# Moving one decode sequence's key pages out of the attention stage and into the chunk stage, with the magnitude on ScalarE

## What is computed

```python
z = einsum('bqhd,bkhd->bhqk', q, k) * SB_SCALE + bias
log_stay = where(valid, log_sigmoid(-z), 0)
log_after = reversed_cumsum(log_stay) - log_stay
a = where(valid, exp(log_sigmoid(z) + log_after), 0);  o = a @ v
```

## Time and profile before

| | us |
|---|---|
| three runs | 1563.23, 1570.99, 1570.99 |
| median | 1570.99 |
| profiled execution, its own time | 1570.6 |
| its span | 1568.9 |
| TensorE busy | 1422.8 (91%) |
| VectorE busy | 790.2 (50%) |
| ScalarE busy | 499.0 (32%) |
| GpSimd busy | 147.2 (9%) |

### The profile page before, as it was taken

The page is one execution under the profiler, slowest core; times in us unless marked ns, Lnnn a source line. Parts: engine busy times, 40 slices in busy tenths (PEclk is TensorE's granted clock), DMA queues, the critical chain, the costliest instruction groups (busy, mean ns, idle before and its releaser), DMA issues.

```text
span 1568.9 us, 28016 instructions
## 1 busy us (share of the span) xinstructions
PE 1422.8 (91%) x10682; PEld 1297.5 (83%) x10682; DVE 790.2 (50%) x2996; ACT 499.0 (32%) x768; POOL 147.2 (9%) x228
## 2 busy tenths in 40 slices
PE   5979978779999888969998899998989999999998
PEld 4979955458988788949776788898989999999997
DVE  4578749986998746553335422234243323332222
ACT  3323343326855322321213433123232222232211
POOL 1000011122320433110330000000000000000000
PEclk9989989889999977876988999998999999999999
DMA  9369846654544200029889998933223333332222
GB/s 323 99 205 291 274 177 201 199 182 146 187 115 115 68 21 21 15 68 267 289 296 310 360 366 294 325 98 126 68 68 92 88 92 93 95 91 82 80 78 75
DMA packets 254474, 252.57 MB, mean 161 GB/s; under 512 B 22433, under 2 KB 215083, under 8 KB 254309
## 3 DMA queue, kind: packets, MB, share of 16 engines
q1 hardware_dynamic: 254341, 250.79, 50.1%
HBM read 235.66 MB, written 15.29 MB: 160 GB/s over the span
## 4 chain that ended last, share of the span: by engine, by line
PE 75%; DVE 11%; ACT 4%; DMA 4%; POOL 2%; issue 2%; SPq 1%; POOLq 0%; DVEq 0%; ACTq 0%
PE ps L1017 53%; PE ps L1046 3%; PE ps L1105 2%; DVE kring L2045 2%; PE ps L1116 2%; PE ps L1390 1%; PE ps L1290 1%; DMA wring<-in_w_ffn_out 1%; PE ps L1307 1%; PE ps L1409 1%; PE ps L1280 1%; PE ps L1294 1%; PE ps L1058 1%; DMA kring<-in_cache_v 1%; SPq L718 1%
## 5 line engine op out<-in xcount | busy, mean ns | idle before, releaser
L1017 PE MATMUL ps<-obT_split,wring_split 128*128 128x268 f32 (+2 forms) x1296 | 264.7, 286 | 0.0
L1017 PE MATMUL ps<-obT_split,qv_split 128*128 128x260 f32 (+2 forms) x1040 | 219.1, 292 | 17.2 <-DVE wring_split L579 15.7
L579 DVE TENSOR_TENSOR wring_split<-wring,vring_split 128x1024 fp32r<-128x1024 f32 (+1 forms) x92 | 110.6, 1202 | 232.5 <-ACT vring_split L573 232.1
L1017 PEld LDWEIGHTS ps<-obT_split,wring_split 128*128 128x128 f32 (+1 forms) x1296 | 201.5, 189 | 0.7
L1017 PE MATMUL ps<-xn_split,vring_split 128*128 128x260 f32 (+1 forms) x960 | 194.6, 284 | 4.1 <-DVE obT_split L593 4.1
L1017 PE MATMUL ps<-obT_split,vring_split 128*128 128x260 f32 (+1 forms) x960 | 197.4, 287 | 0.8 <-issue 0.8
L1017 PEld LDWEIGHTS ps<-obT_split,qv_split 128*128 128x128 f32 (+1 forms) x1040 | 162.2, 190 | 41.6 <-issue 37.4
L1017 PE MATMUL ps<-xn_split,qv_split 128*128 128x260 f32 (+2 forms) x912 | 186.6, 286 | 0.0
L1577 ACT ACTIVATE R<-ps 128x520 f32<-128x520 f32 (+1 forms) x86 | 52.5, 611 | 375.5 <-PE ps L1017 375.5
L579 DVE TENSOR_TENSOR wring_split<-wring,qv_split 128x1024 fp32r<-128x1024 f32 (+1 forms) x73 | 91.8, 1258 | 146.0 <-ACT qv_split L573 145.9
L1017 PEld LDWEIGHTS ps<-xn_split,vring_split 128*128 128x128 f32 x960 | 149.0, 190 | 4.8 <-issue 4.2
(11 more groups left out here) (387 smaller groups left out, 2185.6 us busy)
## 6 DMA issues: line engine op xcount, KB each, us to landing
kring<-in_cache_k SPq DMA_DIRECT2D x74, 512.0 KB, 4.9
wring<-in_w_in SPq DMA_DIRECT2D x72, 512.0 KB, 5.3
vring<-in_cache_v SPq DMA_DIRECT2D x64, 512.0 KB, 6.1
kring<-in_cache_v SPq DMA_DIRECT2D x64, 512.0 KB, 5.5
wring<-in_w_ffn_in SPq DMA_DIRECT2D x44, 512.0 KB, 3.9
vring<-in_cache_k SPq DMA_DIRECT2D x30, 512.0 KB, 4.9
R<-in_cache_k SPq DMA_DIRECT2D x24, 512.0 KB, 6.8
wring<-in_w_ffn_out SPq DMA_DIRECT2D x16, 512.0 KB, 4.1
```

Source lines behind the costliest of these rows:

```text
L579: nc.vector.tensor_tensor(fr(w_part(wlo[:, p % RING, :], p)), w_part(wring[:, p % RING, :], p), w_part(w_high(p), p), ALU.subtract).then_i ...
L1017: last = mm(ps[0:m, 2 * (t % 2) + i, 0:n], fr(w), fr(x[k][:, a + i * n:a + i * n + n]), start=(k == 0 and w is w_h and x is hi), stop=(k = ...
```

## The change

Sequences 1 to 5 go by the plan, so that the attention scores 30 pages instead of 44 and segment 4 none. The seventh sequence (b = 6) is scored inside the chunks on VectorE, at places named in `CHUNK_PAGES`; its query is broadcast into `wring` slot 1 and its pages land in slots 2, 3 and 0, after the last tile of segment 4 has used them. The three weight tiles that would have been prefetched there are loaded after the sequence's last page is scored. The magnitude in the attention becomes an Abs on ScalarE.

```diff
-K_PLAN += [(("att", i), 3 - (i % 4 == 3)) for i in range(2 * H)]
+K_PLAN += [(("att", i), 2 - (i % 8 == 7)) for i in range(2 * H)]
 K_PLAN += list(zip([(2, q) for q in range(4)], (2, 0, 3, 3))) + list(zip([(3, q) for q in range(4)], (2, 2, 2, 2)))
-K_PLAN += list(zip([(4, q) for q in range(4)], (1, 1, 0, 0)))
+K_CHUNKS = PAGES * (DB - 2)
 K_END = PAGES * (DB - 1)
-assert _n == K_END
+assert _n == K_CHUNKS
+
+CHUNK_PAGES = {("levels", 0, 0): [0], ("levels", 0, 1): [1], ("levels", 0, 2): [2, 3], ("kv", 0): [4],
+               ("levels", 1, 1): [5], ("levels", 1, 2): [6, 7], ("levels", 2, 1): [8], ("levels", 2, 2): [9, 10],
+               ("kv", 2): [11], ("levels", 3, 1): [12], ("levels", 3, 2): [13, 14], ("kv", 3): [15]}
@@ k_slot, k_view
+    if n >= K_CHUNKS:
+        return (n - K_CHUNKS) % 3
+            if n >= K_CHUNKS:
+                return wring[:, (2, 3, 0)[k_slot(n)], :]
@@ SP
-                if p == 6 and b + 2 < DB:
+                if p == 6 and b + 3 < DB:
                     spread_q(b + 1)
+            def chunk_query():
+                sp.wait_ge(w_used, done(T_Z - 1))
+                sp.dma_start(wring[:, 1, :], qdram[DB - 2:DB - 1, :].to_broadcast([P, D])).then_inc(qb_in[DB % 2], 16)
+            def chunk_pages(a, b):
+                for p in range(a, b):
+                    k_page(DB - 2, p)
-                    if T_SEG + t + 3 < T_O:
+                    if T_SEG + t + 3 < T_Z or s >= 5 and T_SEG + t + 3 < T_O:
                         w_load(sp, T_SEG + t + 3)
                 if s == 4:
+                    chunk_query()
+                    chunk_pages(0, 3)
                     get_inverse(1)
+                    chunk_pages(3, 6)
                     late_query()
                     get_inverse(2)
+                    chunk_pages(6, 8)
+                    late_page(0)
+                    chunk_pages(8, 10)
                     last_inverse()
-                    late_page(0)
                     get_inverse(3)
+                    chunk_pages(10, 14)
                     late_page(1)
+                    chunk_pages(14, PAGES)
                     late_page(2)
+                    sp.wait_ge(k_used, K_END)
+                    for p in range(T_Z, T_Z + 3):
+                        w_load(sp, p)
                     v_quad(0)
@@ ScalarE, attend
                 def softplus(h):
+                    act.wait_ge(s_z, h + 1)
+                    if h:
+                        act.wait_ge(s_sp, h)
+                    go(es, zs[h % 3], ACT.Abs).then_inc(s_abs, 1)
                     act.wait_ge(s_abs, h + 1)
                     go(es, es, ACT.Exp, scale=-1.0).then_inc(s_exp, 1)
@@ ScalarE and GpSimd, first chunk
-                        act.wait_ge(k_used, K_END)
+                        act.wait_ge(k_used, K_CHUNKS)
-            pool.wait_ge(k_used, K_END)
+            pool.wait_ge(k_used, K_CHUNKS)
@@ VectorE, attend
-                    v.scalar_tensor_tensor(es, zs[h % 3], -1.0, zs[h % 3], ALU.mult, ALU.max).then_inc(s_abs, 1)
-                    for b, p in K_PAGES["att", 2 * h]:
-                        k_page(b, p)
-                    if h + 2 < H:
-                        magnitude(h + 2)
-                    for b, p in K_PAGES["att", 2 * h + 1]:
+                    for b, p in K_PAGES["att", 2 * h] + K_PAGES["att", 2 * h + 1]:
                         k_page(b, p)
@@ VectorE, chunks: levels(c)
+                    pages("levels", c, 0)
                     for g in G2:
                         after("pe", c, "up", 32, g)
                         ue, te = odd(U[:, hs(g), :], 32), even(T[:, hs(g), :], 32)
                         v.tensor_tensor(ue, ue, product(g, 32, 0), ALU.subtract).then_inc(g_dve, 1)
                         v.tensor_tensor(te, te, product(g, 32, 256), ALU.subtract).then_inc(g_dve, 1)
+                        pages("levels", c, 1 + g)
+                def pages(*key):
+                    for p in CHUNK_PAGES.get(key, ()):
+                        k_page(DB - 2, p)
@@ VectorE, chunks: loop over c
+                    pages("kv", c)
                     for g in G2:
                         after("pe", c, "kv", g)
```

More of the change, by code:

```diff
@@ L2043, in k_page @@
                     kh = k_head(n, h)
-                    qh = key_columns(0)[:, h, :] if n >= K_END else qbc[:, b % 2, h * P:h * P + P]
+                    if n >= K_END:
+                        qh = key_columns(0)[:, h, :]
+                    else:
+                        qh = (qbc[:, b % 2, :] if n < K_CHUNKS else wring[:, 1, :])[:, h * P:h * P + P]
                     m = v.tensor_tensor_reduce(kh, kh, qh, 1.0, 0.0, ALU.mult,
@@ L2093, in attend @@
             def attend():
-                def magnitude(h):
-                    dve.wait_ge(s_z, h + 1)
-                    if h == 0:
-                        dve.wait_ge(k_out[0], 16 * 8)
-                        dve.wait_ge(k_out[1], 16 * 4)
-                    if h >= 1:
-                        dve.wait_ge(s_sp, h)
-                    v.scalar_tensor_tensor(es, zs[h % 3], -1.0, zs[h % 3], ALU.mult, ALU.max).then_inc(s_abs, 1)
                 def softplus(h):
@@ L2113, in attend @@
                 for h in (0, 1):
-                    magnitude(h)
                     softplus(h)
```

## The result

The changed kernel took **1551.69 us** (median of 8 runs, 1549.70 to 1557.36); the kernel before, timed beside it, 1563.44 us (8 runs, 1560.78 to 1570.99). The ratio is 0.9914, with a 95% interval of 0.9887 to 0.9941: 11.8 us by the medians, 13.4 by the ratio. Timed once more as one of the experiments, it came to 0.9921 [0.9895, 0.9947].

What follows compares the result with a forecast made beforehand. It took TensorE to bound the kernel (75% of the span), with time to be had only where it stands still. From 1570.6 us, -11.2 - 1.1 - 3.0 + 2.7 = -12.6 gave 1558.0 us, range 1549 to 1571.

Steps and rivals of the forecast that it cites:

- Terms 1 and 2: Attention: fewer pages and the magnitude on ScalarE bring six turns from 91.63 to 80.4 us, -11.2 us.
- the ring: Attention: one head's loop through VectorE, GpSimd, ScalarE and TensorE to the next head's subtraction, 13.4 us instead of 15.27.
- the slack of 1.5 us on both engines: Attention: VectorE and ScalarE would each finish a head's work 1.5 us before the next subtraction is due.
- rival A: Attention: the clock falls anyway and turns stay at about 15.3 us; 1569.2 us, no change; chance 0.10.
- term 1: Attention: pages per head fall from 5.5 to 4, freeing at least 10.2 us of VectorE over six turns.
- Term 3: Start of attention: the first mask shortens once VectorE's magnitude goes, -1.1 us (bounds 0.3 and -1.4).
- Term 4: Fifth weight segment: two pages of the seventh sequence leave VectorE, -3.0 us (bounds -2.0 and -3.6).
- the cap is TensorE's longer wait: Fifth weight segment: the gain could not exceed TensorE's longer wait for VectorE's low parts, 3.6 us.
- Term 5: Chunks: sixteen pages enter VectorE's waits, some reduces slowed by GpSimd's multiplies, +2.7 us, +2.5 of it in chunk 0.
- B: Chunks: page loads come late and VectorE sits waiting at a page; 1572.5 us at worst; chance 0.17.
- C: Chunks: all pages land whole on the chain, 27.2 us in place of 2.7; 1582.5 us, slower; chance 0.08.
- D: Attention: the magnitude's move does nothing because ScalarE becomes the late engine; 1558 to 1568 us; chance 0.05.

Runs made afterwards that it cites:

- e10: The kernel before with only the magnitude moved to ScalarE, plus unread matmuls in TensorE's attention waits (two calls for heads 0 to 5, five after); 1553.04 us.
- e11: The changed kernel with the magnitude back on VectorE, plus unread matmuls in TensorE's attention waits (two calls for heads 0 to 5, five after); 1552.50 us.
- e2: The changed kernel with the magnitude back on VectorE, so only the pages are moved; 1554.30 us.
- e1: The kernel before with only the magnitude moved to ScalarE, all pages left in their places; 1554.72 us.
- e3: The changed kernel with 28 instead of 30 pages in the attention and two back in segment 4; 1556.64 us.
- e8: The kernel before with only the magnitude moved to ScalarE, plus too many unread matmuls in TensorE's attention waits (six calls, twelve for the last two heads); 1577.09 us.
- e4: The changed kernel with one reduce instead of eight for each page in the chunks, all loads and waits kept; 1547.83 us.
- e5: The whole changed kernel timed once more, as one of the experiments; 1551.23 us.
- e9: The changed kernel plus unread matmuls in TensorE's attention waits (two calls for heads 0 to 5, five for 6 and 7); 1546.36 us.
- e6: The changed kernel with chunk pages from page 3 on one place later and the first value pages' loads ahead of the three weight loads; 1550.73 us.
- e12: The changed kernel with chunk pages from page 3 on one place later, plus unread matmuls in TensorE's attention waits (two or five calls); 1545.34 us.

## Why the prediction was right, and where it was off

It said 1558.0 us (1549 to 1571) and faster; it was 1551.7 and faster. The change was foreseen at -12.6 us and is -11.8 by the medians, -13.4 by the ratio. The 6.3 us between 1558.0 and 1551.7 are almost all in the base: **the sum was made against the profiled execution of 1570.6 us, which the prediction took to stand 0.4 us under the median**. With eight runs instead of three the median was 1563.4. From there, -12.6 gives 1550.8.

The nearness of -12.6 is in part luck. With the sizes that are found below (attention -9.9, start -1.9, segment 4 -4.7, chunks +3.8) the sum is -12.7: four terms were off by 0.8 to 1.7 us each, and the errors cancel. The sizes come from single traces, and the kernel before has only the trace of a long execution, so this sum is no proof of the time either.

*Terms 1 and 2, attention: -11.2, and -11.4 in the trace.* The turn of the ring, the slack of 1.5 us on both engines, Abs at 1.32 us without a table load, the 2.21 us of idle and the 2.82 us product all stand in the rows. Two things were not seen. The two parts are not needed together: each alone gives turns of 13.36 to 13.9 us (e10, e11). And the fast product after 2.21 us is not certain, as "every turn is the 13.4 one with the idle of 2.21 and the fast L1116" had it: 7 of 42 were slow, at some 1.55 us each, so that the term in a mean execution is nearer -9.9 (one slow product in six). That is a part of rival A, which was given as all or nothing. One sum of term 1 is too small, though nothing was built on it: the plan takes ten pages out of the six turns, 17 us and not "at least 6 x 1.70 = 10.2"; with six magnitudes that is 26.3 us, and VectorE's busy time fell by 86.04 - 60.74 = 25.3.

The Trainium skill (TensorE: Matmul & The Clock Gate, A second HAM failure mode: psum-queue depth-cycling) describes a neighbouring case: in a bf16 kernel that cycles through PSUM banks, frequent short idles between groups of matmuls make the clock go back and forth between its two levels. Here the idle is a wait for ScalarE's exponential, in fp32, and the trace agrees: 2.21 us of idle in each turn and the clock lost in some. That it is the idle that does it is shown by the filled kernels.

*Term 3, start: -1.1, and -2.0.* The mask fell to 1.19 us as foreseen. The first subtraction starts at 227.40 to 227.86 us in the three traces with the magnitude on VectorE (before, e2, e11) and at 225.03 to 227.06 in the eleven with it on ScalarE, 1.9 us apart on average. So the term was 0.8 us too small by the averages; what the rest consists of was not followed.

*Term 4, segment 4: -3.0, and -4.7 in this pair of traces.* The step that failed there is "the cap is TensorE's longer wait", with "late next is VectorE still, for the last tile". Both waits went. The parts: the second page with its scaling 2.0 us, as worked out. The loads, foreseen "some 1 us sooner", came 1.0 us sooner in SP's queue and 1.9 us sooner in landing. VectorE's first elimination step follows the start of its last L579 by 469.27 - 467.13 = 2.14 us instead of 485.37 - 480.50 = 4.87; these 2.7 us and the 2.0 make 4.7. So "by itself it saves nothing" was right for the first page's reduces, and its place in the DMA queues was the larger part.

The other traces bear this out, with smaller numbers. In the five kernels with two pages in segment 4 (before, e1, e3, e8, e10) the step comes 5.2 to 6.5 us after the last matrix's issue, in the nine without 4.3 to 4.8. TensorE's waits for the low parts there are 4.9, 2.9, 3.6, 3.2 and 2.8 us, 3.5 on average, and none in the nine: the trace of before shows the largest. But in e1, e8 and e10 the clock also fell to its lower level (0.51) within 1.2 us of that wait's end, for 6.9, 6.9 and 3.5 us, and in no kernel without these pages did it fall there. The prediction had put the clock at nothing in this term.

*Term 5, chunks: +2.7, and +3.4 in chunk 0, +0.4 behind it (e4 against after).* L2318 is 1.7 us later in the trace, not 2.5. But the page ahead of the first state update and the clock between add to it: against kernels without pages in the chunks (e1, e10: 36.2) the change needs 39.9 to 41.0 us, so 3.7 to 4.8; against the trace before, 3.4. The mechanism is the one named, five reduces blocked where the prediction counted the multiplies that meet a page; that page 0's would not be waited for was right, that pages 2 and 3's would be as well. The Trainium skill (SBUF — State Buffer, Who interferes with whom) has the rule that a VectorE instruction with two inputs in SBUF contends with a GpSimd one that reads SBUF, over a port pair that is locked. The trace agrees: each stretched reduce takes 1.29 to 1.40 us, the length of one multiply (2.59 us for two). No page load is late but for 1.4 us, once.

*Rivals.* A came true in part, for one turn in six. B did not: VectorE waited 1.4 us for a page in the chunks in all. C is out: it wanted 27.2 us and 3.8 were paid. D is out: ScalarE has 1.45 us left, and its Abs takes 1.32. The chances of the outcomes were added slightly off: 0.60 and a third of B and D are 0.67, not 0.68, and A and the rest of B and D 0.25, not 0.23.

## What to carry to other kernels

Before a sum is hung on the one profiled execution, compare that with the lowest of the runs, not only with the median of three: here it was 7 us off, half the effect. A load that is not waited for still costs, if it stands in the queue ahead of one that is; count its landing time, not only its issue. Where TensorE has a short wait in a repeated turn, cheap matmuls into a free bank can be worth a good part of what the change itself gives: four pairs differ by 4.6 (e5, e9), 2.9 (e1, e10), 3.0 (e2, e11) and 5.1 us (e6, e12), each pair timed in two jobs. But measure one call's length first.

## What the runs showed of the hardware

The clock after a short wait is not settled by the code or by the length of the wait. The same code gave a product of 2.82 us and of 3.98 to 4.51 us after the same 2.21 or 2.25 us of idle; after 4.76 us it was slow 14 times of 14; with 0.38 to 1.03 us of idle left it was fast 32 times of 32. In the kernel before it was fast three times after 2.21 us and slow three times after 3.89 to 4.22. Between kernels with the same idle the work ahead of the product is the same too.

The chunk stage has two lengths: 110.2 to 110.9 us from the first to the fifth state update, or 116.5, in 3 of the 14 traces, with the granted clock at 0.70 instead of 1.00 in chunk 3. Nothing between was seen. This and the slow products are of the size of the scatter between runs of one kernel (5 to 10 us); that they are its whole cause is likely but was not shown, since only one execution of each kernel has a trace.
